# Loading and summing layer 1's gate-and-second-shift modulation group in layer 1's merge

## The reference

```python
for l in range(2):
    mod = silu(c) @ w_mod[l] + b_mod[l]              # 6 x 1024 for the latent tokens
    mod_c = silu(c_ctx) @ w_mod[l] + b_mod[l]        # and for the context
    sh1, sc1, gt1, sh2, sc2, gt2 = split(mod, 6)
    h = rmsnorm(x, g_pre1[l]) * (1 + sc1) + sh1      # the context alike
    y, y_c = token_mixers(h, hc, ...)                # attention, neighbourhood attention, mLSTM, gated merge
    x = x + gt1 * rmsnorm(y, g_post1[l])
    h2 = rmsnorm(x, g_pre2[l]) * (1 + sc2) + sh2
    x = x + gt2 * rmsnorm(expert_choice_ffn(h2, ...), g_post2[l])
    if l == 0: ...                                   # the context stream takes the same two steps
return x
```

## Time and profile before

| | before |
|---|---|
| time of the kernel, median of 3 runs | 1790.78 us (1790.21 to 1791.82) |
| profiled execution, first to last instruction | 1789.8 us |
| PE busy | 1612.4 us, 90% of the span |
| DVE / ACT / POOL busy | 640.9 / 345.1 / 264.0 us |
| weights and other data moved | 530.12 MB, mean 296 GB/s |

### The profile page before, as it was taken

One profiled execution on the slowest core, in us unless ns is written; L12 is line 12 of the kernel. 1 busy time (PEld: TensorE's weight loads), 2 busy tenths in 40 slices (PEclk: granted clock), 3 DMA queues, 4 the chain that ended last, 5 costly groups with the idle time before them and its releaser, 6 DMA issues.

```text
span 1789.8 us, 23904 instructions
## 1 busy us (share of the span) xinstructions
PE 1612.4 (90%) x9908; PEld 949.4 (53%) x9908; DVE 640.9 (36%) x1203; ACT 345.1 (19%) x886; POOL 264.0 (15%) x295
## 2 busy tenths in 40 slices
PE   8999999999999999989889999999998667676776
PEld 4656577777785433324223587688975222232233
DVE  2865455677753213112020555363231110010101
ACT  3223445111132100100001422542220000000001
POOL 4202422344200000000120002235500000000000
PEclk9999999999999999999999999999999886686799
DMA  9525005254699999999999754233799999999997
GB/s 366 196 94 173 1 24 189 94 212 166 226 394 346 407 423 421 421 421 421 413 408 421 275 177 127 82 119 126 264 379 401 420 421 421 421 421 421 421 420 294
DMA packets 134899, 530.12 MB, mean 296 GB/s; under 512 B 10245, under 2 KB 72875, under 8 KB 80265
## 3 DMA queue, kind: packets, MB, share of 16 engines
q1 hardware_dynamic: 131916, 525.15, 74.3%
q0 software_dynamic: 2816, 3.45, 0.9%
q10 hardware_dynamic: 60, 0.02, 0.0%
HBM read 527.48 MB, written 1.09 MB: 295 GB/s over the span
## 4 chain that ended last, share of the span: by engine, by line
PE 66%; DMA 29%; DVE 3%; ACT 1%; issue 1%; DVEq 0%; SPq 0%; ACTq 0%
DMA ring<-in_w_e_dram 29%; PE ps L1441 13%; PE ps L1082 11%; PE ps L1722 11%; PE ps L1554 5%; PE ps L1752 4%; PE ps L1500 4%; PE ps L974 3%; PE ps L1654 2%; PE ps L1372 2%; PE ps L1157 2%; PE ps L1282 2%; PE ps L1682 1%; PE ps L1394 1%; PE ps L995 1%
## 5 line engine op out<-in xcount | busy, mean ns | idle before, releaser
L1722 PE MATMUL ps<-ring,arena 128*32 128x256 f32 (+1 forms) x2800 | 367.4, 507 | 81.2 <-DMA ring<-in_w_e_dram 79.3
L1722 PEld LDWEIGHTS ps<-ring,arena 128*32 128x32 f32 (+1 forms) x2800 | 121.7, 128 | 305.5 <-issue 156.3
L1752 PE MATMUL ps<-ring,arena 128*32 128x256 f32 (+1 forms) x1456 | 199.1, 529 | 68.6 <-DMA ring<-in_w_e_dram 68.4
L1752 PEld LDWEIGHTS ps<-ring,arena 128*32 128x32 f32 (+1 forms) x1456 | 64.4, 133 | 197.9 <-issue 96.8
L1811 ACT ACTIVATE arena<-ps 128x256 f32<-128x256 f32 (+4 forms) x227 | 97.3, 437 | 309.7 <-PE ps L1441 170.2
L2745 DVE COPY arena<-ps 32x512 f32<-32x512 f32 (+1 forms) x120 | 66.4, 554 | 252.8 <-PE ps L1752 251.6
L2729 DVE TENSOR_TENSOR arena<-arena,ps 128x512 f32<-128x512 f32 (+1 forms) x32 | 17.7, 555 | 370.8 <-PE ps L1722 370.8
L2152 ACT ACTIVATE arena<-ps 128x512 f32<-128x512 f32 (+1 forms) x32 | 15.7, 490 | 677.2 <-PE ps L1722 677.2
L1441 PE MATMUL ps<-arena,ring 128*128 128x128 f32 (+1 forms) x728 | 127.7, 321 | 0.0
L1082 PE MATMUL ps<-arena,ring 128*128 128x512 f32 (+1 forms) x352 | 120.4, 497 | 0.0
L1441 PEld LDWEIGHTS ps<-arena,ring 128*128 128x128 f32 x728 | 109.5, 191 | 19.3 <-issue 11.5
(11 more groups left out here) (302 smaller groups left out, 1913.5 us busy)
## 6 DMA issues: line engine op xcount, KB each, us to landing
ring<-in_w_e_dram SPq DMA_DIRECT2D x355, 1024.0 KB, 15.3
ring<-in_w_in_dram SPq DMA_DIRECT2D x42, 1024.0 KB, 9.7
ring<-in_w_mod_dram SPq DMA_DIRECT2D x32, 1024.0 KB, 7.4
arena<-in_w_e_dram SPq DMA_DIRECT2D x20, 1024.0 KB, 9.0
ring<-in_w_mod_dram SPq DMA_DIRECT2D x16, 512.0 KB, 10.5
ring<-in_w_out_dram SPq DMA_DIRECT2D x8, 1024.0 KB, 10.6
arena<-in_w_mod_dram SPq DMA_DIRECT2D x8, 1024.0 KB, 14.2
arena<-in_w_br_ml_dram SPq DMA_DIRECT2D x8, 512.0 KB, 5.6
```

Source lines behind the costliest of these rows:

```text
L1722: mm = pe.matmul(ps[M * j:M * j + M, m, 0:NW], XSTs[l][e // GROUP % 2][:, kk, e % GROUP, 0:M], w[:, k, j * NW:(j + 1) * NW], start=kk == 0 ...
L1752: mm = pe.matmul(ps[M * j:M * j + M, y_bank, 0:NW], hidTs[l][:, (kk % nb) * P + (kk // nb) * M:(kk % nb) * P + (kk // nb) * M + M], w[:, k ...
```

## The change

The eight loads of group (1, 1) move from layer 0's queue into layer 1's ring, one after each of the units 1, 3, ..., 15 of layer 1's merge, and DVE sums them there, after `gated(u)` of the same unit, into `X`'s context rows (`first_acc[1][1]`). PE sums over the partitions behind unit 16 and turns the row behind unit 18. The numbers 4 and 5 of the groups change places, so that (1, 2) is summed first. All that `mod4` did in layer 0 is gone: loads, 32 DVE pieces, the sum, the row, the turn, and the waits for them. SP's order changes in three places: layer 0's first expert load for the ring goes ahead of the two `gate1` loads; in layer 1 the spare places `mixer_consts` and `held` are filled ahead of the branch weights; and the ring's first expert loads go ahead of `ctx_rows` and `gate1`. POOL loads the bias and gain rows for the group just before the merge of layer 1.

```diff
-MOD_GROUPS = [(l, g) for l in range(2) for g in range(3)]
+MOD_GROUPS = [(0, 0), (0, 1), (0, 2), (1, 0), (1, 2), (1, 1)]
...
-SUMMED = [{2: 6, 3: 15}, {}]
-FIRST_GROUP = (1, 5)
+SUMMED = [{2: range(6, 14), 3: range(15, 23)}, {5: range(1, 17, 2)}]
+FIRST_GROUP = (1, 4)
...
     if l == 0:
-        mods = [(("mod4", l, k), None) for k in range(KD)]
-        order += mods[:4] + [(("gate1", l), None)] + ring[:3] + mods[4:] + pick(SPARE_ORDER[0]) + ring[3:7] + pick(SPARE_ORDER[1]) + ring[7:]
+        order += ring[:1] + [(("gate1", l), None)] + ring[1:3] + pick(SPARE_ORDER[0]) + ring[3:7] + pick(SPARE_ORDER[1]) + ring[7:]
         return order
-    return order[:-4] + pick(SPARE_ORDER[2][:3]) + order[-4:] + [(("gate1", l), None)] + pick(SPARE_ORDER[2][3:]) + ring[:3] + pick(SPARE_ORDER[3]) + \
+    at = order.index((("branch", l, 0), None))
+    return order[:at] + pick(SPARE_ORDER[2][:2]) + order[at:] + ring[:1] + pick(SPARE_ORDER[2][2:3]) + [(("gate1_row", l), None)] + \
+        pick(SPARE_ORDER[2][3:4]) + ring[1:2] + [(("gate1", l), None)] + ring[2:3] + pick(SPARE_ORDER[2][4:]) + pick(SPARE_ORDER[3]) + \
         ring[3:7] + pick(SPARE_ORDER[4]) + ring[7:]
...
                 elif name[:3] == "mix" and name[3:].isdigit():
                     sp.wait_ge(sem("mg_branch"), before("mg_branch", l) + 24)
-                    if l == 0:
-                        sp.wait_ge(sem("mod_part"), 3 * KD + 4 + int(name[3:]) + 1)
...
                     if n == EARLY:
+                        if l:
+                            pool.wait_ge(sem("weight_sums"), before("weight_sums", l) + 4 * EARLY)
+                            mod_rows(5)
                         pool.wait_ge(sem("attn_v"), before("attn_v", l) + len(layers[l].units) // 2)
...
-                if l:
-                    keep_clock(5, 7)
-                else:
-                    pe.wait_ge(sem("mod_part"), 4 * KD)
-                    pe.wait_ge(sem("mod_row"), 4)
-                    for j in range(4):
-                        mm = pe.matmul(ps[32 * j:32 * j + 32, 6, :], pick[:, 1, :], mod4_acc[j], start=True, stop=True)
-                    mm.then_inc(sem("mod_summed"), 1)
+                keep_clock(5, 7 if l else 1)
...
                 for j, t in enumerate(L.chunks[:-1]):
-                    if l == 0:
-                        for k in ((0, 1, 2, 3), (4, 5), (6, 7))[j]:
-                            mod4_part(k)
                     post1(j, t)
```

More of the change, by code:

```diff
@@ L108, in before @@
     return LAYER0[name] * l
-SUMMED = [{2: 6, 3: 15}, {}]
-FIRST_GROUP = (1, 5)
+SUMMED = [{2: range(6, 14), 3: range(15, 23)}, {5: range(1, 17, 2)}]
+FIRST_GROUP = (1, 4)
 FIRST_SUMMED = [[(0, 1), (), (2,), (3, 4, 5), (6, 7), (), ()], [(), (0, 1, 2), (3, 4), (5,), (6, 7), (), ()]]
 def mods_summed(l, u):
-    return [(o, u - first) for o, first in SUMMED[l].items() if first <= u < first + KD]
+    return [(o, units.index(u)) for o, units in SUMMED[l].items() if u in units]
 HALVES = (range(4), range(4, 8))
@@ L214 @@
           26: "mix3", 29: "merged_end", 32: "ya1", 35: "gains", 38: "held", 41: "params", 44: "xst1"}]
-SPARE_ORDER = [[120, 56, 72, 88, 104, 20, 136], [23, 3, 14, 17, 152, 40, 26], [2, 5, 38, 8, 11], [14, 20, 23, 26], [29, 32, 17, 35, 41, 44]]
+SPARE_ORDER = [[120, 56, 72, 88, 104, 20, 136], [23, 3, 14, 17, 152, 40, 26], [5, 38, 2, 8, 11], [14, 20, 23, 26], [29, 32, 17, 35, 41, 44]]
 SLOT_OF, PREVIOUS, USE = [], [], []
 def _assign_slots():
-    turn, last, count = 0, {}, {f"mix{i}": 2 for i in range(4)}
+    turn, last, count = 0, {}, {}
     for l in range(2):
@@ L437, in backbone @@
         hots, Srs, Sgs = ([view(20480 + 512 * b, 2, 2, P), view(19200 + 256 * b, 1, 2, P)] for b in range(3))
-        mod4_acc = [view(at, 512) for at in (13312, 13824, 21504, 22912)]
         XTs = [view(8192, 4, KD, P), view(6144, 4, KD, P)]
@@ L574, in spare_free, with gate1_row @@
                     sp.wait_ge(sem("wo_ready"), before("wo_ready", l) + 4 * layers[l].nt)
+            def gate1_row(l):
+                sp.wait_ge(sem("mod_row"), 6 if l else 2)
+                for s in layers[l].streams:
+                    sp.dma_start(gates1[l, s].rearrange("(h n) -> h n", h=2), gate_row(l, 1)[s:s + 33:32, :])\
+                        .then_inc(sem("gates1_stored"), 16)
             def load(n, dst, src):
@@ L1022, in merge_mods @@
                     mod_turn(FIRST_GROUP[l])
-                for o, first in SUMMED[l].items():
-                    if u == first + KD:
-                        mod_sum(o, mod_acc)
-                    if u == first + KD + 2:
+                for o, units in SUMMED[l].items():
+                    if u == units[-1] + 1:
+                        mod_sum(o, first_acc[1] if l else mod_acc)
+                    if u == units[-1] + 3:
                         mod_turn(o)
@@ L1648, in gather @@
                         s = L.streams[si]
-                        if l == 0 and g == 0 and s:
-                            pe.wait_ge(sem("mod_row"), 5)
                         for i in range(4):
@@ L1771, in _ @@
                     if at == 1 and g:
-                        if l == 0 and g == 1:
-                            pe.wait_ge(sem("mod_col"), 5)
                         scatter(g - 1)
@@ L1779, in _ @@
                         turn_gates(g)
-                        if l == 0 and g == 0:
-                            mod_turn(4)
                     if e == N_EXP - 1:
@@ L2064, in _ @@
                         mod_cols(FIRST_GROUP[l])
-                    if l == 0 and u == 17:
-                        mod_cols(2)
+                    if u == (19 if l else 17):
+                        mod_cols(5 if l else 2)
                 exp_ln()
@@ L2175, in _ @@
                         gates_turned(g)
-                        if l == 0 and g == 0:
-                            mod_cols(4)
                 def post_last(j):
@@ L2267, in mod_part @@
                         ins = dve.tensor_scalar(acc[s], w_slot(n), cT[:, k, s:s + 1], None, ALU.mult)
-                ins.then_inc(sem("mod_part"), 1)
-            def mod4_part(k):
-                s_ = f"mix{k % 4}"
-                w = spare_slots[s_]
-                dve.wait_ge(sem(f"weights_landed_{s_}"), 16 * (k // 4 + 1))
-                dve.wait_ge(sem("mod_part"), 3 * KD + k)
-                for j in range(4):
-                    cols = slice(512 * j, 512 * j + 512)
-                    if k:
-                        ins = dve.scalar_tensor_tensor(out=mod4_acc[j], in0=w[:, cols], scalar=cT[:, k, 1:2], in1=mod4_acc[j],
-                                                       op0=ALU.mult, op1=ALU.add)
-                    else:
-                        ins = dve.tensor_scalar(mod4_acc[j], w[:, cols], cT[:, k, 1:2], None, ALU.mult)
                 ins.then_inc(sem("mod_part"), 1)
@@ L2556, in gated @@
                             own(ins)
-                    if l == 0 and u == 15:
-                        mod_row(2)
+                    if u == (17 if l else 15):
+                        mod_row(5 if l else 2)
                 def mods(u):
```

33 lines of the change are left out of this document (9 added, 24 removed).

## The result

The changed kernel takes 1799.06 us (1797.83 to 1799.27, 4 runs) beside 1790.49 us (1790.15 to 1791.82, 4 runs) of the kernel before: ratio 1.0044, 95% interval 1.0032 to 1.0056, so **slower by about 8.6 us**. Two repeats, each with a fresh set of runs of before, gave 1.0032 (1.0019 to 1.0044) and 1.0034 (1.0021 to 1.0047). All 14 runs of the changed kernel lie between 1794.88 and 1799.46 with a median of 1798.01; the four later sets of before have medians of 1791.2 to 1791.5. The better figure is therefore about +6.7 us. The forecast was +4.2 and 1795.0, range to 1798.2: the right sign, but too small. The first median lies outside the range; that of all 14 runs lies just inside its upper end, which is no credit to the sum, since it had 4.2 for what is 6.7.

The account below looks back on a forecast made before the run. The prediction took the DMA weight queue to bound the expert stages and PE to bound layer 1's merge. Layer 0 0, merge start 2.8 and steps 1.4 gave +4.2 us, 1795.0 us, range 1791.6 to 1798.2.

Parts of the forecast that it names:

- Layer 0 is worth 0: Layer 0's queue: removing eight loads gains 0, since the 21 places limit the loads; bounds -0.5 and +0.5 us.
- The start of the merge, +2.8: Layer 1's merge before the first step: PE's added waits for DVE's parts 0 and 1 cost 2.8 us.
- Part 0 at 1.28: Start of layer 1's merge: DVE's part 0 takes 1.28 us, from the `X` row of L2267.
- `gated(2)`'s 1.16: DVE's list at the merge's start: `gated(2)` takes 0.42 and a middle value of 0.74, together 1.16 us.
- the gaps, taken at +0.2: DVE's list at the merge's start: gaps of 0.04 between seven instructions add 0.2 us.
- Rival 2: Layer 1's merge: DVE and POOL contend, lengthening part 1 and some steps; +2.3 to +4.9, 1797.3 to 1799.9 us; chance 0.13.
- The sign that I named: Layer 1's merge: PE waiting for DVE's L2246 in unit 5, first step 2 to 4 us later, would show the forecast right.
- The steps, +1.4: Layer 1's merge steps: DVE's parts are hidden, PE's sum and turn are not, costing 1.4 us.
- The queue, hidden: Layer 1's DMA queue: the output projection's weights and `gate1` still land in time, by some 10 us; no cost.
- 1 (lighter chain): Merge's start: DVE's chain is lighter, gatings at 0.42; +2.9 us, time 1793.7; chance 0.22.
- 3 (faster by layer 0): Layer 0's queue not dry at 559.58, so the eight loads' 20.1 us are saved; time 1774.9; chance 0.05.
- 4 (only 1.4 us): Merge's start covered by another wait, so only 1.4 us remain; time 1792.2; chance 0.09.

Follow-up runs that it names:

- filled_wait: Changed kernel plus 9 and 4 unused matrix products on PE ahead of units 3 and 4 of layer 1's merge; 1797.39 us, ratio 1.0029.
- filled_again: Repeat of filled_wait, the changed kernel with PE's waits filled by unused products, beside the unaltered changed kernel in one batch; 1797.03 us.
- pool_after_part: Changed kernel, with POOL's sums for layer 1's first step waiting until DVE's part 0 is done; 1798.42 us, ratio 1.0035.
- loads_back: Changed kernel, with the eight 1 MB loads issued again in layer 0, unused, at their old place; 1796.87 us, ratio 1.0029.
- small_parts: Changed kernel, with the group's DVE parts multiplying only 32 of 2048 columns; 1794.62 us, ratio 1.0018.
- thin_pool: Changed kernel, with POOL's four sums at the start of layer 1's merge taking 8 of each 128 columns; 1793.9 us, ratio 1.0016.
- late_parts: Changed kernel, with the parts at units 7 to 13 and 15 of layer 1's merge, none ahead of the first step; 1795.09 us, ratio 1.0020.
- parts_5_to_19: Changed kernel, with parts behind units 5, 7, ..., 19, then sum, row and turn behind 20, 21 and 22; 1793.12 us, ratio 1.0007.
- thin_sum: parts_5_to_19, with PE's sum reading 32 of each 512 columns and its turn one transpose, not four; 1791.63 us, ratio 1.0001.

## Why the prediction was right or wrong

All versions read by the same sum, start and steps against before's 8.18 and 78.83:

| kernel | start | steps | sum of both differences | measured |
|---|---|---|---|---|
| after, three profiles | 13.44, 13.24, 11.63 | 80.49 | +6.9, +6.7, +5.1 | +6.7 (14 runs) |
| filled_wait, filled_again | 11.65, 11.64 | 80.49 | +5.1 | +6.1, +5.8 |
| pool_after_part (the first step's first products slow, 3.10 us in place of 1.95) | 13.04 | 81.64 | +7.7 | +7.1 |
| loads_back | 12.05 | 80.49 | +5.5 | +5.6 |
| small_parts | 9.41 | 80.49 | +2.9 | +3.1 |
| thin_pool | 9.47 | 80.49 | +3.0 | +2.6 |
| late_parts | 8.18 | 82.93 | +4.1 | +3.8 |
| parts_5_to_19 | 8.18 | 80.49 | +1.7 | +1.6 |
| thin_sum | 8.18 | 79.34 | +0.5 | +0.1 |

The sums of the profiled executions hold within 1 us of the measured medians (but for the third profile of after, 1.6 under), so nothing larger is missing; what is left over, up to 1 us, I can't assign.

**Layer 0 is worth 0: right.** The end of layer 0's experts moved by no more than the run's offset, and putting the loads back made nothing slower. The reason given, places and not transfers set the pace at 555, is what the trace shows. One limit of it: I had only shown that the queue was dry, not how much room it had.

**The start of the merge, +2.8: the step that failed.** I had the mechanism and the list of DVE instructions; it measured +3.5 by DVE alone and +3.5 to +5.3 with the clock. Two terms failed:
- *Part 0 at 1.28.* The row came from a place where POOL does nothing. Here POOL sums weights, and part 0 took 2.38, 1.1 more. (`gated(2)`'s 1.16 then came out at 0.84, since POOL's sum had ended by then, which gave 0.3 back; the gaps, taken at +0.2, came out at -0.1, another 0.3; and PE's stop ahead of its last products added the rest, some 0.25.) Rival 2 named the cause and put it on the wrong instructions: it charged the parts with two SBUF inputs in the steps, but the six parts in the steps took 2.35 to 2.38; where one met POOL, POOL had come second and waited (1.71 to 2.84 us for a sum of 1.27). The prediction's "as each of these parts has" is wrong for part 0: it multiplies one tensor by a column, so it has one large input, and it was the one hit. The Trainium skill (SBUF — State Buffer, Who interferes with whom) says that the port pair shared by VectorE and GpSimd is an exclusive lock, held for a whole instruction, and that a DVE instruction takes part in it either with two SBUF inputs, against a GpSimd instruction that reads SBUF, or in a two-port performance mode. The Trainium skill (GPSIMD Engine Reference, Specifications), which I quoted, names both cases too, and I used one. The traces agree with both cases and, to within 0.2 us, with whole instructions taking turns: 32 columns took 1.32 us, ending with POOL's sum; and `gated`'s first product (L2514), with one of its two inputs in PSUM, stayed at 0.42 beside POOL.
- *The clock.* No step of mine asked what PE's waits do to PE's clock. With 2.11 and up to 0.88 us of waiting close together the granted clock fell, and 16 products took up to 6.68 us in place of 3.72. It did so in all three profiles of the changed kernel and in that of `loads_back`, whose merge has the same work (start 12.05): PE was busy for 2.0 to 2.6 of the 5 us from 1215, and the clock over the 16 products was 0.54, 0.55, 0.79 and 0.68. It stayed at 1.00 in `small_parts` and `thin_pool`, with waits of 0.9 to 1.1 us and PE busy for 3.6 and 4.0 of these 5 us. Much of the slowness is hidden behind part 1, so the net cost is 0 to 1.8 us. The Trainium skill (TensorE: Matmul & The Clock Gate, Part 1: The HAM clock gate) says that an idle PE stands at half its clock, 1.2 GHz, and that the point at which it gets the full clock varies from run to run. The four profiles agree in that it varies; that it falls in a stretch where PE has work and only stops twice is from these rows alone. The sign that I named, PE's wait for L2246 in unit 5, does not show in the changed kernel's trace, where the slow products cover it; with the waits filled it is there, 0.90 us.

**The steps, +1.4: right in kind, 1.66 measured.** The turn cost 0.46 as priced. The sum cost 1.08 where I had 0.91 (2.81 us between two products, where 1.73 is usual), and the product behind it took 0.1 more. That one part hides in a step was right, and late_parts showed the edge: with two in a step PE waits.

**The queue, hidden: right.** No PE wait for a weight or `gate1`. DMA still falls to 0.67 where layer 1's experts begin: this execution is 6.2 us later there, and its 1351.2 to 1356.2 answers to 1345 to 1350 of before. The last stage kept its length: 442.2 us from the issue at 1353.75 to the end, 442.2 from 1347.57 before.

**Rivals.** 1 (lighter chain), 3 (faster by layer 0) and 4 (only 1.4 us) fell. Rival 2's time, 1797.3 to 1799.9, holds the measured one, and its cause is a part of the miss, but it did not act in the steps, where I had put it: that its time was met is luck. Of the miss of 2.5 us (4.2 against 6.7), 0.7 is DVE's list and 0.3 the steps. The other 1.5 falls to the clock (0 to 1.8 in the profiles) and to something that stays unassigned: with the waits filled and the clock at 1.00, the time is still 0.7 to 1.0 above its sum.

## What to carry to other kernels

When an instruction is put into an engine's list, take its length from a row with the same neighbours: here a neighbour on POOL added 1.1 us to 1.28. A wait added to a matrix engine that was near full can cost more than its own length, since the clock may fall behind it, as in four profiles here; so price a new wait in a full stretch with that too, or fill it with products as `filled_wait` does. And before moving a load to save transfer time, find what starts the next load: as long as places set it, the bytes are free, up to a room. Count it in bytes against the best rate, also behind the point where the queue first runs dry: here that came to some 13 MB.

## What the runs showed of the hardware

- A DVE instruction with all in SBUF (TENSOR_SCALAR with one tensor, SCALAR_TENSOR_TENSOR with two) that starts while POOL sums in SBUF waits for the end of POOL's instruction: TENSOR_SCALAR 128x32 took 1.32 us, 128x2048 2.38 in place of 1.28, SCALAR_TENSOR_TENSOR 128x2048 3.23 and 3.32 in place of 2.35. POOL's sum that comes second waits likewise: 2.13 in place of 1.33.
- After PE's waits of 2.11 and 0.88 us the granted clock was 0.53 from 1220 to 1225 and 1.00 again from 1225. The same program had 0.50 and 0.80 in that stretch in two other executions. With the waits filled by products it was 1.00.
- Between executions of one kernel in one batch (4 to 27 of them) the time spread by 1.4 to 4.8 us, more than I took for it from three runs.
